# Block 2 of a two-block transformer kernel: scores of split q and k taken earlier, av projected last, two evictions moved to ScalarE

## The chip, the cores and the metric

One core of one Trainium2 chip runs the whole program. The metric is the time of one execution on the device, in microseconds. PE is TensorE, DVE VectorE, ACT ScalarE, POOL GpSimd and SP the engine whose queue issues the weight loads.

## The reference

Two blocks of two layers each work on x (512 tokens, 1024 features), in float32. The first block is not touched by the change. A layer of the second block is, cut to what matters:

```python
def hybrid_layer(x, mem, norm_g, w_in, w_out, mem_norm_g, w_mem_kv, qk_g):
    h = rms_norm(x, norm_g)
    proj = jnp.einsum('btd,de->bte', h, w_in)
    a_q, a_k, a_v, a_g, b_q, b_k, b_v, b_g, m_q, m_g = jnp.split(proj, cuts, axis=-1)
    qa = rope(rms_norm(to_heads(a_q, 6), qk_g[0])); ka = rope(rms_norm(to_heads(a_k, 6), qk_g[1]))
    oa = from_heads(moba_attention(qa, ka, to_heads(a_v, 6)))      # causal at 512 tokens
    ...                                                            # b: dilated, 6 heads, the same
    m_k, m_v = jnp.split(rms_norm(mem, mem_norm_g) @ w_mem_kv, 2, axis=-1)
    om = from_heads(memory_attention(qm, km, to_heads(m_v, 4)))    # 256 memory rows, 4 heads
    y = jnp.concatenate([oa * silu(a_g), ob * silu(b_g), om * silu(m_g)], axis=-1)
    return x + jnp.einsum('bte,ed->btd', y, w_out)
```

A head has 64 features. Scores are q k^T / 8 with a mask, then softmax, then times v.

## The kernel before

Every engine has its program written out by hand, and semaphores join them. There is no scheduler: what an engine does next is the next line of its own loop.

**Projections.** Each weight group (aq, ak, av, bq, bk, bv, mq, ag, bg, mg, and the two halves of out) has 8 steps of 128 input features. A step takes one slot of a ring of 4 (`RING`): SP loads the raw weights, ACT rounds them to w_hi (`round_weights`, L1021), DVE subtracts to w_lo (`residue`, L1343), and PE does three float32r passes (hi by hi, hi by lo, lo by hi) for each of the 2 to 4 banks of the group (`step`, L695). ACT and DVE run up to 3 steps ahead (`AHEAD`) and then wait for PE to free a slot. A group's banks have to be read (evicted) before the next group starts in them.

**Order of the projections in block 2.** `block_2` of PE projects aq, ak, av, bq, and then bk with `gemm_led`, which puts the first events of the attention (`a.lead`) between its steps. DVE works on the heads of aq and ak (norm, rotation: `head_norm`, `rotate`, L1442) beside av and bq, evicts ak and bq, and, within the attention, bv and mq (L1383). ACT evicts aq, av, bk (L1059) and the gates ag, bg, mg.

**Attention of block 2.** `Stream` holds its order. There are 8 pairs of heads: 3 of moba (a), 3 of dilated (b), 2 of memory. A pair has 4 units, one for each 128 queries: unit i of a causal pair has i + 1 blocks of 128 keys, one of memory always has 2. A unit takes 1 or 2 steps of two key blocks, so a causal pair has 6 steps, a memory pair 4, and the whole 44. In a step PE does the events of `begin`, then its share of the projections still to do (bv, mq, ag, bg, mg, 5 steps of out: `side`), then, at a pair's first step, the product with v of the pair before (`values`, L791), then the transposes of the step's probabilities (`turn_probs`, L779), for which there is one PSUM bank (T_BANK).

The events are: `turn`, where PE transposes q and k of a pair into banks 0 and 1 (L750) and DVE copies them out (L1478, L1482); `scores`, where PE multiplies them into the same two banks, one a head (L762), DVE masks and takes the maximum (L1498), and ACT takes the exponential (L1068); and `scale`, where DVE multiplies by the inverse sum (L1510). Scores of a unit come two steps ahead of its first step, and there are 3 buffers of probabilities.

The scores are plain float32 matmuls over all 128 rows: `kT_2` holds each head's k in its own 64 rows, with zeros (written once by POOL) in the other 64, and q of both heads stands in qT. A float32 matmul stands in the trace as two records.

## Time and profile before

| what | us |
|---|---|
| three runs | 1687.91, 1688.66, 1690.15 |
| median | 1688.66 |
| the profiled execution | 1690.31 |
| its span in the trace | 1688.5 |
| its mean granted clock | 0.993 of full speed |

The profile is of one execution. Its page gives the busy time of the engines and the costliest groups of instructions. Other views give the same for a stretch of time, list who waited for whom, or show the instructions in order of time. A busy time counts overlapping matmuls once in a stretch but each in full in a group, since the end of a matmul is modelled; what a matmul takes of PE's time is read from one start to the next. Block 2 runs from about 1070 us to the end, its first layer up to about 1385 us.

### The profile page before, as it was taken

Reading aid. Unit: us, or ns where it says so; the run is one execution under the profiler, and the core shown is the slowest. Engines: PE = TensorE matmul, PEld = TensorE weight load, DVE = VectorE, ACT = ScalarE, POOL = GpSimd, SP = SyncE. Lnnn points to the kernel's source line nnn. Section 1 sums busy time; section 2 is a strip of 40 time slices with the busy share of each in tenths; the row PEclk is TensorE's granted clock in tenths of the full one; section 3 lists DMA queues with packets and bytes.
Section 4 is the critical chain, followed back from the end, with each engine's and each line's share of the span. In section 5 each row is a group of like instructions: output and inputs, shape, how many; then the busy total and the mean of one; then the engine's idle time right before and its main releaser. Section 6 shows DMA issues by size and latency. Waiting matters only on the chain.

```text
span 1688.5 us, 21496 instructions
## 1 busy us (share of the span) xinstructions
PE 1618.3 (96%) x8009; PEld 1326.6 (79%) x8009; DVE 1005.9 (60%) x2246; ACT 729.7 (43%) x1503; POOL 57.8 (3%) x80
## 2 busy tenths in 40 slices
PE   6999999999999999999999999999989999998999
PEld 6878777788887878777788887999767789985667
DVE  4597656444444397757443344486876554788663
ACT  4444443333234443543332434434456553354662
POOL 0000002000001000002000001000000010000000
PEclk9999999999999999999999999999999999999999
DMA  6332121323323223112233323332112233211121
GB/s 219 93 92 71 42 63 51 100 88 100 100 94 96 85 87 88 51 50 63 76 96 92 99 90 110 104 88 60 57 38 69 76 95 92 83 56 38 38 76 62
DMA packets 80883, 136.23 MB, mean 81 GB/s; under 512 B 8190, under 2 KB 33420, under 8 KB 80780
## 3 DMA queue, kind: packets, MB, share of 16 engines
q1 hardware_dynamic: 77264, 129.48, 25.7%
q10 hardware_dynamic: 3516, 5.37, 1.0%
q8 instruction: 64, 1.05, 0.3%
q14 instruction: 39, 0.32, 0.1%
HBM read 132.74 MB, written 2.10 MB: 80 GB/s over the span
## 4 chain that ended last, share of the span: by engine, by line
PE 46%; DVE 13%; ACT 4%; issue 2%; POOL 0%; ACTq 0%; DVEq 0%
PE gemm_bank L695 35%; PE aux_bank L762 3%; PE aux_bank L791 3%; DVE w_lo L1343 2%; PE aux_bank L779 2%; DVE rope L1442 1%; DVE head_sums L1395 1%; ACT w_hi L1021 1%; DVE probs L1498 1%; ACT probs L1068 1%; DVE kT L1482 1%; PE aux_bank L750 1%; DVE probs L1510 1%; ACT L1296 0%; PE aux_bank L939 0%
## 5 line engine op out<-in xcount | busy, mean ns | idle before, releaser
L1021 ACT ACTIVATE w_hi<-raw 128x512 fp32r<-128x512 f32 (+3 forms) x524 | 305.5, 587 | 673.3 <-PE gemm_bank L695 671.9
L1343 DVE TENSOR_TENSOR w_lo<-raw,w_hi 128x512 fp32r<-128x512 f32 (+3 forms) x524 | 329.9, 636 | 441.9 <-ACT w_hi L1021 440.2
L695 PE MATMUL gemm_bank<-act_hi,w_hi 128*128 128x512 f32 x768 | 316.7, 412 | 10.9 <-DVE mq_flat L1383 3.7
L695 PE MATMUL gemm_bank<-act_hi,w_lo 128*128 128x512 f32 x768 | 300.2, 391 | 0.0
L695 PE MATMUL gemm_bank<-act_lo,w_hi 128*128 128x512 f32 x768 | 299.9, 391 | 0.0
L695 PE MATMUL gemm_bank<-w_hi,act_hi 128*128 128x384 f32 (+3 forms) x736 | 269.3, 366 | 6.4 <-DVE bq L1383 2.9
L695 PE MATMUL gemm_bank<-w_lo,act_hi 128*128 128x384 f32 (+3 forms) x736 | 257.2, 349 | 0.0
L695 PE MATMUL gemm_bank<-w_hi,act_lo 128*128 128x384 f32 (+3 forms) x736 | 257.2, 349 | 0.0
L695 PEld LDWEIGHTS gemm_bank<-act_hi,w_hi 128*128 128x128 f32 x768 | 144.6, 188 | 47.9 <-issue 12.7
L695 PEld LDWEIGHTS gemm_bank<-act_lo,w_hi 128*128 128x128 f32 x768 | 144.8, 189 | 31.9 <-issue 2.9
L695 PEld LDWEIGHTS gemm_bank<-act_hi,w_lo 128*128 128x128 f32 x768 | 144.5, 188 | 31.0
L695 PEld LDWEIGHTS gemm_bank<-w_hi,act_hi 128*128 128x128 f32 x736 | 139.2, 189 | 24.2 <-issue 10.0
L695 PEld LDWEIGHTS gemm_bank<-w_lo,act_hi 128*128 128x128 f32 x736 | 139.2, 189 | 11.3 <-issue 1.9
L695 PEld LDWEIGHTS gemm_bank<-w_hi,act_lo 128*128 128x128 f32 x736 | 138.8, 189 | 9.7
L762 PE MATMUL aux_bank<-kT,qT 128*128 128x256 f32 (+7 forms) x384 | 121.4, 435 | 5.8 <-DVE kT L1482 4.8
L1082 ACT ACTIVATE probsT<-aux_bank 128x256 f32<-128x256 f32 (+1 forms) x136 | 71.9, 529 | 114.7 <-PE aux_bank L779 113.9
L1068 ACT ACTIVATE probs<-probs,neg_max 128x128 f32<-128x128 f32 (+2 forms) x192 | 104.2, 544 | 35.6 <-DVE neg_max L1498 35.2
L779 PE MATMUL aux_bank<-ident,probs 128*128 128x128 f32 x464 | 76.1, 280 | 14.3 <-DVE probs L1510 14.2
L762 PEld LDWEIGHTS aux_bank<-kT,qT 128*128 128x128 f32 (+1 forms) x384 | 64.3, 194 | 27.3 <-DVE kT L1482 9.2
L779 PEld LDWEIGHTS aux_bank<-ident,probs 128*128 128x128 f32 x464 | 56.5, 142 | 36.9 <-DVE probs L1510 21.0
L695 PE MATMUL gemm_bank<-y_hi,w_hi 128*128 128x512 f32 x192 | 74.8, 390 | 0.3 <-ACT gate L1201 0.3
L695 PE MATMUL gemm_bank<-y_hi,w_lo 128*128 128x512 f32 x192 | 74.7, 389 | 0.0
(289 smaller groups left out, 2132.7 us busy)
## 6 DMA issues: line engine op xcount, KB each, us to landing
raw<-in_w_in SPq DMA_DIRECT2D x104, 512.0 KB, 3.5
raw<-in_w_in SPq DMA_DIRECT2D x64, 384.0 KB, 3.3
raw<-in_w_out SPq DMA_DIRECT2D x32, 512.0 KB, 3.7
raw<-in_w_branch SPq DMA_DIRECT2D x24, 512.0 KB, 3.7
raw<-in_w_mem_kv SPq DMA_DIRECT2D x8, 512.0 KB, 3.8
raw<-in_w_in SPq DMA_DIRECT2D x16, 256.0 KB, 2.8
raw<-in_w_in SPq DMA_DIRECT2D x8, 416.0 KB, 4.8
x<-in_x SPq DMA_DIRECT2D x4, 512.0 KB, 5.2
```

The costliest lines, as they stand in the source:

```text
L695: last = pe.matmul(o, a, c, start=begin and n == 0, stop=end and n == 2)
L750: last = pe.transpose(bank[0:kind.rows, t * P:(t + 1) * P], of(h, t), ident[:, :])
L762: pe.matmul(bank[:, 0:n_keys * P], a.qT_of(g, x)[:, i * P:(i + 1) * P], a.kT_of(g, x)[:, 0:n_keys * P], start=True, stop=True).then_inc(fu ...
L779: last = pe.transpose(bank[:, c:c + P], probs[a.where][m % 3][:, x, j * P:(j + 1) * P], ident[:, :])
L791: last = pe.matmul(bank[x * HD:(x + 1) * HD, kind.first_i(j) * P:T], kind.v_of(a.head(g, x), j), a.probsT_of(g, x, j), start=(j == 0), sto ...
L1021: act.activation(w_hi[:, s % RING, 0:n], raw[:, p % RAW, kk % PIECE, 0:n], ACT.Copy)\
L1068: act.activation(rows, rows, ACT.Exp, bias=neg_max[:, c:c + 1], scale=-1.0, accum_out=row_sum[:, c:c + 1]).then_inc(probs_ready, 1)
L1082: act.activation(a.turned_to(m, j0, j1), bank[:, 0:2 * (j1 - j0) * P].rearrange("p (x j s) -> p x j s", x=2, s=P), ACT.Copy)\
L1343: dve.tensor_tensor(w_lo[:, s % RING, 0:n], raw[:, p % RAW, kk % PIECE, 0:n], w_hi[:, s % RING, 0:n].bitcast(F32), ALU.subtract).then_inc( ...
L1395: dve.tensor_reduce(head_sums[:, c:c + heads], sq[:, n % 2, 0:heads, 0:d], AX_X, ALU.add)\
L1442: mark(dve.tensor_tensor(tmp[i][:, :, :, :], xx, t4, ALU.mult))
L1482: ins = dve.tensor_copy(a.kT_of(g, x + hh)[r, 0:kind.k_tiles * P], bank[r, 0:kind.k_tiles * P])
```

## The change

1. **Scores.** ACT rounds the transposed q and k of a pair from PSUM into `q_hi` and `k_hi` (`turned_hi`), DVE subtracts to `q_lo` and `k_lo` (event `low`, one step after `turn`), both float32r. PE does three float32r passes for each head, each over the head's own 64 rows (`scores_2`), the two heads taking turns. `kT_2`, its zeros and the semaphore `keys_zeroed` go.
2. **Two units at once.** Units 0 and 1 of a causal pair, and each two units of a memory pair, put their scores side by side in one bank (`together`).
3. **When.** Scores of block 2 come 4 steps ahead (`SCORES_LEAD`), or as soon as their buffer of probabilities is free; there are 4 buffers. `turn` moves to other steps.
4. **Projections.** The order is aq, ak, bq, bk, av; the lead events stand in av (turn in its step 3, scores in 5). DVE and ACT begin on the heads of b beside av.
5. **Evictions.** bq, bv and mq are evicted by ACT, not by DVE.

```diff
-        two("av", 2 * WA, WA)
         two("bq", 4 * WA, WB)
         two("bk", 4 * WA + WB, WB)
+        two("av", 2 * WA, WA)
...
             for m, mine in enumerate(self.steps_of):
                 self.begin[mine[0]].insert(0, ("scale", m))
-                if mine[0] >= 2:
-                    self.begin[mine[0] - 2].append(("scores", m))
+                if mine[0] >= 2 and self.together(m):
+                    last = max(self.together(m)) - self.buffers
+                    free = self.steps_of[last][-1] + 1 if last >= 0 else 0
+                    self.begin[max(mine[0] - SCORES_LEAD[block], free, 0)].append(("scores", m))
...
-        a.lead = {4: [("turn", 0, 0)], 5: [("scores", 0)], 6: [("scores", 1)]}
-        for g, (at_pair, step) in {1: (0, 1), 2: (0, 3), 3: (2, 1), 4: (2, 3), 5: (3, 3), 6: (4, 3), 7: (5, 3)}.items():
+        a.lead = {3: [("turn", 0, 0)], 4: [("low", 0, 0)], 5: [("scores", 0)]}
+        for g, (at_pair, step) in {1: (0, 0), 2: (0, 5), 3: (1, 5), 4: (2, 5), 5: (3, 5), 6: (4, 5), 7: (5, 4)}.items():
...
+        def scores_2(a, m):
+            g, kind = m // NT, a.kind(m)
+            if m % NT == 0:
+                aux_wait_read(pe, a.key("q", g, 0))
+                aux_wait_read(pe, a.key("k", g, 0))
+            banks = [aux_open(a.key("S", m, x), S_BANKS[x]) for x in range(2)]
+            for mm, c in a.together(m).items():
+                i, keys = mm % NT, kind.n_keys(mm % NT) * P
+                for n, (qq, kk) in enumerate(((q_hi, k_hi), (q_lo, k_hi), (q_hi, k_lo))):
+                    for x in range(2):
+                        r = slice(x * HD, (x + 1) * HD)
+                        last = pe.matmul(banks[x][:, c:c + keys], qq[r, g % 2, i * P:(i + 1) * P],
+                                         kk[r, g % 2, 0:keys], start=n == 0, stop=n == 2)
+                        if n == 2 and mm == max(a.together(m)):
+                            last.then_inc(full_of(a.key("S", m, x)), 1)
...
+        def turned_hi(a, g):
+            for what, hi in (("q", q_hi), ("k", k_hi)):
+                bank = aux_wait_full(act, a.key(what, g, 0))
+                n = T if what == "q" else a.pairs[g][0].k_tiles * P
+                act.activation(hi[:, g % 2, 0:n], bank[:, 0:n], ACT.Copy).then_inc(turned_hi_ready, 1)
...
+            for n, (what, hi, lo) in enumerate((("q", q_hi, q_lo), ("k", k_hi, k_lo))):
+                key = a.key(what, g, 0)
+                columns = T if what == "q" else a.pairs[g][0].k_tiles * P
+                dve.wait_ge(turned_hi_ready, 2 * a.turn_count(g) - 1 + n)
+                dve.tensor_tensor(lo[:, g % 2, 0:columns], aux_bank[aux_place[key][0]][:, 0:columns],
+                                  hi[:, g % 2, 0:columns].bitcast(F32), ALU.subtract).then_inc(read_of(key), 1)
...
+                elif name in ("bv", "mq"):
+                    evict_now(gi, ACT.Copy, lambda b: flat_2(name)[:, b, :])
```

**PE where the attention starts** (first layer: last matmuls of the led projection, then step 0). `aq` and `ak` are the operands of the second pair's turn. Before:

```order
L695 MATMUL gemm_bank<-w_lo,act_hi 128x384
L695 MATMUL gemm_bank<-w_hi,act_lo 128x384
L762 MATMUL aux_bank<-kT_177,qT_175 128x384 x2
L695 MATMUL gemm_bank<-w_hi,act_hi 128x384
L695 MATMUL gemm_bank<-w_lo,act_hi 128x384
L695 MATMUL gemm_bank<-w_hi,act_lo 128x384
L695 MATMUL gemm_bank<-w_hi,act_hi 128x384
```

and the turn of the second pair, a step later, behind the first transposes of probabilities:

```order
L695 MATMUL gemm_bank<-w_lo,act_hi 128x384
L695 MATMUL gemm_bank<-w_hi,act_lo 128x384
L779 MATMUL aux_bank<-ident,probs_181 128x128 x2
L750 MATMUL aux_bank<-ident,aq 128x128 x4
L750 MATMUL aux_bank<-ident,ak 128x128 x4
L695 MATMUL gemm_bank<-w_hi,act_hi 128x384
```

Now:

```order
L717 MATMUL gemm_bank<-w_lo,act_hi 128x384
L717 MATMUL gemm_bank<-w_hi,act_lo 128x384
L803 MATMUL aux_bank<-k_hi,q_hi 128x384 x2
L803 MATMUL aux_bank<-k_hi,q_lo 128x384 x2
L803 MATMUL aux_bank<-k_lo,q_hi 128x384 x2
L803 MATMUL aux_bank<-k_hi,q_hi 128x512 x2
L803 MATMUL aux_bank<-k_hi,q_lo 128x512 x2
L803 MATMUL aux_bank<-k_lo,q_hi 128x512 x2
L772 MATMUL aux_bank<-ident,aq 128x128 x4
L772 MATMUL aux_bank<-ident,ak 128x128 x4
L717 MATMUL gemm_bank<-w_hi,act_hi 128x384
L717 MATMUL gemm_bank<-w_lo,act_hi 128x384
```

The scores of unit 2 (384 keys), those of unit 3 (512 keys) and the second pair's turn now stand behind each other with nothing between; all three use banks 0 and 1.

**DVE at the end of the heads of a** (first layer; `ISA` of L1452, now L1512, tells PE that the heads are ready; `sq` holds the squares of heads of b). Before:

```order
L1447 TENSOR_TENSOR ak<-rope_170,rope_171 128x24x32
L1452 ISA
L1343 TENSOR_TENSOR w_lo<-raw,w_hi 128x384 x3
L1383 COPY bq<-gemm_bank 128x384 x4
L1343 TENSOR_TENSOR w_lo<-raw,w_hi 128x384 x4
L1478 COPY qT_175<-aux_bank 128x512
L1482 COPY kT_177<-aux_bank 64x512 x2
L1343 TENSOR_TENSOR w_lo<-raw,w_hi 128x384
```

Now:

```order
L1507 TENSOR_TENSOR ak<-rope_170,rope_171 128x24x32
L1512 ISA
L1403 TENSOR_TENSOR w_lo<-raw,w_hi 128x384 x4
L1455 TENSOR_REDUCE head_sums<-sq_172 128x6
L1403 TENSOR_TENSOR w_lo<-raw,w_hi 128x384
L1455 TENSOR_REDUCE head_sums<-sq_172 128x6
L1403 TENSOR_TENSOR w_lo<-raw,w_hi 128x384
L1455 TENSOR_REDUCE head_sums<-sq_172 128x6
L1403 TENSOR_TENSOR w_lo<-raw,w_hi 128x384
L1455 TENSOR_REDUCE head_sums<-sq_172 128x6
L1546 TENSOR_TENSOR q_lo<-aux_bank,q_hi 128x512
L1546 TENSOR_TENSOR k_lo<-aux_bank,k_hi 128x512
```

The eviction of bq and the three copies of q and k are gone, the sums of the heads of b have come in between, and two subtractions stand where the copies were.

**ACT within the attention** (first layer, around the end of the projection mq). Now:

```order
L1064 ACTIVATE w_hi<-raw 128x384 x2
L1120 ACTIVATE probs_185,row_sum<-probs_185,neg_max 128x384 x2
L1137 ACTIVATE probsT_188<-aux_bank 128x2x2x128
L1102 ACTIVATE mq_flat<-gemm_bank 128x256 x4
L1064 ACTIVATE w_hi<-raw 128x384
L1108 ACTIVATE q_hi<-aux_bank 128x512
L1108 ACTIVATE k_hi<-aux_bank 128x512
L1137 ACTIVATE probsT_188<-aux_bank 128x2x256
```

Before, `mq_flat` was DVE's to write, and ACT had neither `q_hi` nor `k_hi`: its rows at the next gate, for comparison, were

```order
L1082 ACTIVATE probsT_185<-aux_bank 128x2x256
L1021 ACTIVATE w_hi<-raw 128x384
L1068 ACTIVATE probs_183,row_sum<-probs_183,neg_max 128x384 x2
L1082 ACTIVATE probsT_185<-aux_bank 128x2x128
L1296 ACT_TABLE_LOAD
L1296 ACTIVATE agT<-gemm_bank 128x512 x3
L1021 ACTIVATE w_hi<-raw 128x384
L1082 ACTIVATE probsT_185<-aux_bank 128x2x2x128
```

The eviction of mq and the rounding of the next pair's q and k now stand ahead of the copy of the step's transposed probabilities.

## Rows read from the trace of the kernel before

**Rows 1.** the page: its span, and the busy time of each engine (us, share, instructions)
```profile
span 1688.5 us, 21496 instructions
PE 1618.3 (96%) x8009; PEld 1326.6 (79%) x8009; DVE 1005.9 (60%) x2246; ACT 729.7 (43%) x1503; POOL 57.8 (3%) x80
```

**Rows 2.** sums by stretch: PE, weight load, DVE, ACT, POOL busy (x count), granted clock
```profile
1180.00:1240.00 60.00, 52.39 (x301) 41.06 (x301) 53.06 (x154) 25.47 (x71) 0.00 (x0) 0.97 0.17 53
1240.00:1300.00 60.00, 57.31 (x290) 40.58 (x288) 39.84 (x117) 37.94 (x88) 0.00 (x0) 1.00 0.16 45
...
1070.00:1688.50 618.50, 582.77 (x3114) 484.91 (x3112) 405.35 (x1059) 294.36 (x694) 5.58 (x14) 0.99 0.23 68
```

**Rows 3.** waits of PE from 1070 us to the end: total us, times, longest
```profile
PE aux_bank L779 <- DVE probs L1510: 12.2, 10, 2.0
PE aux_bank L762 <- DVE kT L1482: 4.8, 10, 0.8
PE gemm_bank L695 <- DVE mq_flat L1383: 3.7, 2, 2.7
...
PE gemm_bank L695 <- DVE bq L1383: 2.9, 2, 1.5
...
PE gemm_bank L695 <- DVE bv L1383: 1.6, 2, 0.8
PE aux_bank L762 <- DVE qT L1478: 1.0, 2, 0.5
```

**Rows 4.** timeline of PE: start, us, line, operation, count; f32 scores, then projection matmuls
```profile
1179.40 1.03 PE L762 MATMUL aux_bank<-kT,qT 128*128 128x256 f32 x4
...
1180.44 0.34 PE L695 MATMUL gemm_bank<-w_lo,act_hi 128*128 128x384 f32 x1
1180.61 0.34 PE L695 MATMUL gemm_bank<-w_hi,act_lo 128*128 128x384 f32 x1
...
1190.86 0.28 PE L695 MATMUL gemm_bank<-w_hi,act_lo 128*128 128x256 f32 x1
...
1191.21 0.28 PE L695 MATMUL gemm_bank<-w_hi,act_lo 128*128 128x256 f32 x1
...
1241.49 0.40 PE L695 MATMUL gemm_bank<-act_lo,w_hi 128*128 128x512 f32 x1
...
1241.95 0.39 PE L695 MATMUL gemm_bank<-act_hi,w_hi 128*128 128x512 f32 x1
```

**Rows 5.** timeline of PE: matmuls with 64-row operands in two halves of the array
```profile
269.29 2.88 PE L929 MATMUL aux_bank<-vc,ks_tok 64*128 64x256 f32 x16 [0.52 <-DVE att L1866]
```

**Rows 6.** timeline of PE: into and out of matmuls with a 16-row operand
```profile
237.31 0.60 PE L779 MATMUL aux_bank<-ident,probs 128*128 128x128 f32 x4
237.84 1.98 PE L857 MATMUL aux_bank<-g_T,w_gu 16*128 16x512 f32 x4
239.74 0.50 PE L695 MATMUL gemm_bank<-w_hi,act_hi 128*128 128x512 f32 x1
240.08 0.40 PE L695 MATMUL gemm_bank<-w_lo,act_hi 128*128 128x512 f32 x1
```

**Rows 7.** groups of DVE, 1070 to 1380 us: count, busy us, mean ns, idle before
```profile
L1482 DVE COPY kT<-aux_bank 64x512 f32<-64x512 f32 x12 | 8.2, 684 | 0.2
L1478 DVE COPY qT<-aux_bank 128x512 f32<-128x512 f32 x8 | 5.5, 686 | 2.6 <-PE aux_bank L750 2.6
L1536 DVE TENSOR_TENSOR x<-gemm_bank,x 128x512 f32<-128x512 f32 x8 | 5.2, 687 | 5.2 <-PE gemm_bank L695 5.2
L1442 DVE TENSOR_TENSOR rope<-bq,table 128x768 f32<-128x768 f32 x4 | 3.6, 951 | 0.0
...
L1383 DVE COPY bq<-gemm_bank 128x384 f32<-128x384 f32 x4 | 1.9, 548 | 0.0
```

**Rows 8.** groups of ACT in the same stretch
```profile
L1082 ACT ACTIVATE probsT<-aux_bank 128x512 f32<-128x512 f32 x32 | 18.8, 589 | 16.8 <-PE aux_bank L779 16.5
...
L1059 ACT ACTIVATE av<-gemm_bank 128x384 f32<-128x384 f32 x4 | 2.0, 492 | 0.1
```

161 lines of the change are left out of this document (89 added, 72 removed).

## The prediction

> **What bounds the kernel now.** I read the page first: PE is busy 1618 of 1688.5 us [rows 1], so a change pays where it takes work off PE or ends a wait of PE. Only block 2 changes, so next comes its stretch, from 1070 us to the end: PE is busy 583 of 618.5 us, and DVE 405 and ACT 294 have room on average [rows 2]. Not everywhere: from 1180 to 1240 us, where DVE rotates the heads of b beside the attention, DVE is busy 53 of 60 us and PE only 52, while in the 60 us after that DVE has 40 and PE 57 [rows 2]. The list of PE's waits names what is late: probabilities that DVE has yet to scale (12.2 us), copies of turned q and k (4.8 + 1.0), evictions by DVE of mq (3.7), bq (2.9) and bv (1.6) [rows 3]. These are 26 us of the 36 in which PE is idle. So there are two places to gain, PE's work and some 26 us of waits, and both go straight to the end, since PE is the chain.
>
> **The scores, before.** Four float32 records of 256 columns (one unit, two heads) and one projection matmul of 384 columns start within 1180.44 - 1179.40 = 1.04 us, and such a projection matmul takes 0.17, so the unit takes 0.87 us, 0.217 a record [rows 4]. It scales with columns. Six causal pairs have 1280 key columns each (128 + 256 + 384 + 512), two memory pairs 1024: 9728 a layer, 38 times 256. Two layers: 76 x 0.87 = 66 us.
>
> **The scores, after.** Float32r matmuls of projections start 0.117 us apart at 256 columns (three in 0.35 us), 0.173 at 384 and 0.23 at 512; transposes with 128 columns and a weight load each, 0.11 [rows 4, 6]. If the two heads, in different halves of the array's rows, run at the same time, three pairs of matmuls take: units 0 and 1 together 3 x 0.11 + 3 x 0.117 = 0.68 us, unit 2 0.52, unit 3 0.69, two memory units 0.70. A layer: 6 x 1.89 + 4 x 0.70 = 14.1; both 28 us.
>
> Do they run together? The trace has one case: 16 float32 records of 256 columns over 64 rows, four in one half, four in the other, and so on, take 2.88 us to the modelled end [rows 5]. One after another they would take 16 x 0.217 plus some 0.16 of tail, 3.6. The 0.75 saved is a whole record at each of the three changes of half, all that this order allows. In the new order the half changes with every matmul, so I take full overlap as likeliest.
>
> **Going in and out of half-array matmuls** has a price. Four transposes of 0.11 us, then four records over 16 rows of 2 x 0.213 us, then one projection matmul of 0.23, would take 0.44 + 1.71 + 0.23 = 2.38 us; from 237.31 to 240.08 they take 2.77 [rows 6]. So 0.4 us a visit. The change makes 3 visits for a causal pair and 2 for a memory pair, 22 a layer, 44 x 0.4 = 17.6 us. The bound below is 0 (all of it hidden by a wait that was there anyway). The Trainium skill's page "TensorEngine Tiling (Array Packing)", Key Properties, says that changing the tiling mode drains TensorE. By that rule, which speaks against this change, each visit costs, and the 0.4 us of the trace agrees with it.
>
> Sum for the scores: 66 - 28 - 17.6 = 20 us gained.
>
> **Waits that go.** (a) bq: after the change ACT evicts it, with nothing in front, where DVE had three w_lo of the next group first; 2.9 us go. (b) The copies of q and k: the turn now stands a step or more ahead of its scores, so rounding (ACT, 2 x 0.59 us [rows 8]) and subtraction (DVE, 2 x 0.69, as for other reads of PSUM with a second operand [rows 7]) have a step of about 4.7 us; 5.8 go. (c) bv and mq, 5.3: ACT evicts them where it now evicts gates. It reads bank 0 while PE fills the others, but exponentials may be in front of it; I leave 1.0, so 4.3 go. (d) Scaled probabilities, 12.2: the longer lead doesn't help where DVE is behind with everything, and the rotation (eight products of 0.95 us a layer [rows 7], and as much again in sums) still lies in 4 steps of the attention, now steps 4 to 8 instead of 9 to 12. DVE has there about 3.8 us of rotation, 1.8 of scores and scaling and 1.2 of w_lo in a step for which PE takes 5. Over a layer DVE gets 10 us lighter: 15.4 of copies (12 x 0.684, 8 x 0.686 and four short ones [rows 7]) and 5.2 of evictions go, 10.5 of subtractions come. I take a quarter, 3.2 us, and leave 9.
>
> **A wait that comes.** At step 0 PE now does the scores of unit 2, of unit 3, and the second pair's turn back to back, all in banks 0 and 1. Behind unit 2's scores PE waits for DVE to read both banks, 2 x 0.6 us plus 0.2 to get there; behind unit 3's for 0.7 + 0.2 until bank 0 is read, and 0.3 more for bank 1 behind the q transposes. With the ends of the matmuls some 2.9 us a layer, 5.8 in all; everything behind it on PE waits too, the fill first, and nothing covers it. Later pairs have two steps between any two users of these banks.
>
> **What costs nothing.** ACT gets 14.4 us a layer (roundings 14 x 0.59 + 2 x 0.38, evictions 8 x 0.49 + 4 x 0.38 [rows 8]). Its fullest stretch has 38 of 60 us [rows 2] and would have 42 of 60: the cover is ACT's slack. POOL's zeros were not waited for. The weight loads of SP keep their sizes and only swap places. Without that cover see rival 3.
>
> **Sum.** -20.2 (scores) - 2.9 - 5.8 - 4.3 - 3.2 + 5.8 = -30.6 us. Against the profiled execution's own 1690.3 us this is 1659.7; it stood 1.6 above the median of the three runs, so **1658 us**, 1.8% faster.
>
> **The rivals.**
>
> 1. *The two heads don't overlap in the array* (float32r over 64 rows could behave otherwise than the float32 of [rows 5]). Then a layer's scores take 6 x 3.78 + 4 x 1.40 = 28.3 us, 57 in two, and with the visits 74 where 66 were: 8 lost instead of 20 gained, 1686 us. For it: no row shows alternation. Against: three changes of half, each with full overlap. 8%.
>
> 2. *Weight loads of the two heads follow each other.* Every matmul has its own load, and no row shows load and matmul of 128 columns below 0.11 us [rows 6]. If two heads' loads can't overlap, a pair of matmuls takes at least 0.22: units 0 and 1 1.32 us, unit 2 0.66, unit 3 0.69, two of memory 1.32, 42.6 us in two layers. The scores then gain 6 instead of 20: 1672 us. For it: one bus could feed both. Against: in [rows 5] the overlap included the loads. 15%. The Trainium skill's page "TensorE: Matmul & The Clock Gate", LDWEIGHTS (loading the stationary operand), lets a load's time go by its columns whatever its rows, at 128 columns 107 ns; a load of 64 rows would be no cheaper, which is what this rival needs, while the trace's 0.11 agrees with the price.
>
> 3. *ACT becomes late, and the kernel slower.* There is one bank for transposed probabilities, so PE's transposes of each step wait for ACT's copy of the step before. Ahead of that copy ACT now has, in some steps, four exponentials at once, two roundings or an eviction. If ACT falls behind by more than a step, PE waits in most of 88 steps; from 0.35 us a step (30.6 / 88) the change loses. At 0.4 us a step it is 35 us: 1693. Against: ACT has 18 of 60 us free even where it is fullest. 7%.
>
> 4. *DVE sets the pace for the first ten steps.* Whatever PE saves there (about a quarter of the scores' gain and of the waits, 7 us a layer) turns into longer waits for scaled probabilities or for w_lo: 1672 us. For it: 53 of 60 us [rows 2], and the rotation in one piece. Against: DVE is 10 us lighter. 14%.
>
> 5. *All goes well*: the 9 us left for probabilities vanish and half the visits are hidden: 1640 us. 6%.
>
> **How the numbers follow.** The forecast has 50%. Its own range is 1648 (visits half free) to 1666 (the start's wait and those for probabilities both 4 us worse). Range: rivals 2 and 4 are taken in, with some room above for both of them at once; 1 and 3, 15%, stay out above, and the far part of 5 below: 1644 to 1681. What this kernel's measurement can tell from no change is about 0.2%, 3.4 us. Faster than 1685.3: forecast, rivals 2, 4 and 5, and a part of 1: 0.88. Within 0.2%: most of 1, 0.05. Slower: 3, and 1 with some of 3, 0.07.
>
> **What the profile after would show.** Right: records of the new score line in pairs that start within some 0.01 us, pairs 0.11 to 0.23 us apart; from the last matmul before such a group to the first after it 0.4 us more than the columns need; no waits of PE for evictions by DVE or for turned q and k; two waits of about 1.4 and 1.1 us at step 0 of each layer; DVE's busy time 20 us lower, ACT's 29 higher; the granted clock no lower than 0.99. Wrong: pairs spread by 0.11 (rival 2) or by their columns (rival 1), PE's transposes waiting for ACT's copy of probsT (rival 3), or more than 12 us of waits for scaled probabilities (rival 4).

## The result, and the profile after

The changed kernel is slower. Its median is **1700.3 us** (1699.0 to 1702.1, four runs) against 1688.7 for the kernel before on the same chip: ratio 1.0068, 95% interval 1.0051 to 1.0086. The forecast was 1658, its range ended at 1681, and 0.07 was left for slower. The profiled execution has 1701.4 us and a span of 1699.6.

The page of the changed kernel, its first lines:

```profile
span 1699.6 us, 21791 instructions
...
PE 1603.0 (94%) x8137; PEld 1315.9 (77%) x8137; DVE 983.7 (58%) x2206; ACT 750.9 (44%) x1559; POOL 55.5 (3%) x79
```

Beside [rows 1] PE has 15 us less work, DVE 22 less, ACT 21 more (20 less and 29 more were forecast for the last two). The work of PE and DVE went about as forecast, ACT's by less, and the span the other way, so the time is in waits. The waits of PE from 1070 us to the end (total us, times, longest), to be laid beside [rows 3]:

```profile
PE aux_bank L803 <- DVE k_lo L1546: 26.5, 12, 5.4
PE aux_bank L822 <- DVE probs L1576: 20.0, 14, 2.1
PE aux_bank L803 <- DVE neg_max L1559: 3.8, 2, 2.5
PE aux_bank L822 <- ACT probsT L1137: 3.3, 6, 0.8
PE gemm_bank L717 <- ACT bgT L1355: 2.1, 2, 1.1
...
PE aux_bank L772 <- DVE neg_max L1559: 1.5, 2, 0.8
```

The evictions of bq, bv and mq are gone from the list. The wait for turned q and k has grown from 5.8 to 26.5 us, that for scaled probabilities from 12.2 to 20.0. The sums by stretch (columns as in [rows 2]) show that no engine is short of time there:

```profile
1180.00:1240.00 60.00, 49.36 (x325) 40.29 (x325) 39.48 (x107) 28.80 (x79) 0.00 (x0) 0.94 0.16 51
1240.00:1300.00 60.00, 48.36 (x273) 34.32 (x270) 37.76 (x122) 33.91 (x82) 0.00 (x0) 0.98 0.14 42
...
1070.00:1688.50 618.50, 559.23 (x3208) 467.47 (x3207) 380.52 (x1016) 315.17 (x750) 5.56 (x14) 0.97 0.22 66
```

DVE has 39 of 60 us where it had 53, and still PE waits for it more. The stretches don't hold quite the same work, since the rotation now begins earlier, but in 20 us pieces too DVE's fullest piece of the attention (1200 to 1220 us) has 16.6 us of work. Now the longest of the twelve waits for k_lo in order of time (start, us, engine, line, idle time before and its releaser; PE's projection matmuls left out):

```profile
1185.47 0.60 PE L772 MATMUL aux_bank<-ident,aq 128*128 128x128 f32 x4
...
1185.90 0.60 PE L772 MATMUL aux_bank<-ident,ak 128*128 128x128 f32 x4
...
1188.95 0.60 PE L822 MATMUL aux_bank<-ident,probs 128*128 128x128 f32 x4
1189.01 0.58 ACT L1108 ACTIVATE q_hi<-aux_bank 128x512 fp32r<-128x512 f32 x1
1189.14 0.42 DVE L1403 TENSOR_TENSOR w_lo<-raw,w_hi 128x256 fp32r<-128x256 f32 x1 [2.04 <-ACT w_hi L1064]
1189.48 3.56 DVE L1502 TENSOR_TENSOR rope<-bq,table 128x768 f32<-128x768 f32 x4
...
1193.54 0.68 DVE L1546 TENSOR_TENSOR q_lo<-aux_bank,q_hi 128x512 fp32r<-128x512 f32 x1
1194.14 0.68 DVE L1546 TENSOR_TENSOR k_lo<-aux_bank,k_hi 128x512 fp32r<-128x512 f32 x1
...
1194.97 0.80 PE L803 MATMUL aux_bank<-k_hi,q_hi 64*128 64x512 f32 x2 [5.42 <-DVE k_lo L1546]
```

The turn ends at 1186.5. ACT rounds q 2.5 us later, since the weights of the step come first and wait for a free slot of the ring. DVE stands idle 2.04 us for the same weights, then does w_lo and 3.56 us of rotation, and only then, at the start of its next step, the subtraction. PE has ended its step at 1189.55; its next begins with the scores of the last unit, which go into the banks that the turn has filled. It stands there 5.42 us, to 1194.97.

### The profile page after: what moved, and what is told of

Same layout as the page of the kernel before. It is cut to its first block, busy times and chain, and to the rows that moved or that the text cites. A ratio compares the mean times of both kernels' runs of the same rounds, so it can differ in the third digit from the quotient of the medians.

```text
span 1699.6 us, 21791 instructions
## 1 busy us (share of the span) xinstructions
PE 1603.0 (94%) x8137; PEld 1315.9 (77%) x8137; DVE 983.7 (58%) x2206; ACT 750.9 (44%) x1559; POOL 55.5 (3%) x79
## 4 chain that ended last, share of the span: by engine, by line
PE 46%; DVE 12%; ACT 4%; issue 2%; POOL 0%; ACTq 0%; DVEq 0%
PE gemm_bank L717 36%; PE aux_bank L834 3%; DVE w_lo L1403 2%; PE aux_bank L822 2%; PE aux_bank L803 2%; DVE rope L1502 2%; ACT w_hi L1064 1%; ACT probs L1120 1%; PE aux_bank L787 1%; PE aux_bank L772 1%; DVE probs L1576 1%; DVE probs L1559 1%; DVE head_sums L1455 1%; DVE q_lo L1546 0%; ACT probsT L1137 0%
## 5 line engine op out<-in xcount | busy, mean ns | idle before, releaser
L717 PE MATMUL gemm_bank<-act_hi,w_hi 128*128 128x512 f32 x768 | 312.3, 407 | 8.5 <-ACT u L1102 3.5
L717 PE MATMUL gemm_bank<-y_lo,w_hi 128*128 128x512 f32 x192 | 74.7, 389 | 0.0
L1576 DVE TENSOR_SCALAR probs<-probs,row_inv 128x128 f32<-128x128 f32 (+2 forms) x192 | 64.5, 379 | 3.4
```

Source lines behind the costliest of these rows:

```text
L717: last = pe.matmul(o, a, c, start=begin and n == 0, stop=end and n == 2)
L1576: ins = dve.tensor_scalar(rows, rows, row_inv[:, c + x:c + x + 1], None, ALU.mult)
```

## The experiments

All ran with the kernel before on the same chip; its medians were 1688.4 to 1689.8. "Waits" are PE's from 1070 us to the end, in one profiled execution each, in us. "Half" is how long the trace's clock records grant half of full speed (1.2 of 2.4 GHz) after 1070 us. It is that of the profiled execution; executions of one kernel differ in it (mean granted clock 0.986 to 0.991 in the four of e2), so a few us of it between two kernels say little. Intervals of kernels less than about 4 us apart overlap (e11 and e9, e15 and e6). The diff of an experiment that is built on another shows only what it adds.

| kernel | median | ratio, interval | q, k | probs | probsT | masks | ACT's evictions | half |
|---|---|---|---|---|---|---|---|---|
| before | 1688.7 | | 5.8 | 12.2 | 3.1 | 0 | 0.9 (DVE's 8.2) | 10 |
| changed | 1700.3 | 1.0051-1.0086 | 26.5 | 20.0 | 3.3 | 5.3 | 2.1 | 34 |
| e1 low in the step of turn | 1677.7 | 0.992-0.995 | 1.9 | 22.0 | 3.3 | 5.3 | 5.6 | 21 |
| e2 last unit a step later | 1678.3 | 0.9923-0.9956 | 12.2 | 13.9 | 7.1 | 5.2 | 2.1 | 18 |
| e3 head by head | 1700.7 | 1.0052-1.0082 | 26.4 | 19.4 | 2.5 | 5.2 | 2.1 | 38 |
| e4 before, ACT evicts bv, mq | 1680.4 | 0.9933-0.9962 | 5.9 | 11.0 | 3.0 | 0 | 0.9 (DVE's 2.9) | 3 |
| e5 e1 + start spread | 1671.1 | 0.988-0.9909 | 2.4 | 19.6 | 3.0 | 0.8 | 5.5 | 18 |
| e6 e1 + scale a step earlier | 1665.7 | 0.9845-0.9878 | 2.7 | 0 | 8.2 | 11.6 | 4.9 | 24 |
| e7 low behind the weights | 1688.4 | 0.9989-1.0008 | 12.3 | 23.2 | 1.7 | 5.3 | 2.1 | 31 |
| e8 e1 + memory heads later | 1674.8 | 0.9903-0.9932 | 6.4 | 15.3 | 1.7 | 5.3 | 5.5 | 27 |
| e9 e5 + e6 + e8 | 1659.1 | 0.9807-0.9843 | 10.6 | 0 | 6.3 | 2.1 | 5.5 | 14 |
| e10 e9, copy first | 1666.1 | 0.9848-0.988 | 10.8 | 0 | 2.0 | 5.9 | 8.4 | 21 |
| e11 e9, roots in pieces | 1656.4 | 0.979-0.9821 | 3.3 | 0 | 3.5 | 2.1 | 3.6 | 17 |
| e12 before, scale earlier | 1686.4 | 0.9973-0.9992 | 11.6 | 0 | 2.8 | 2.8 | 0.9 (DVE's 10.8) | 7 |
| e13 e11, memory heads only | **1652.5** | 0.9764-0.9796 | 7.3 | 0 | 6.3 | 2.1 | 5.5 | 7 |
| e14 e1 with two steps of lead | 1668.8 | 0.9859-0.9888 | 7.2 | 12.3 | 4.9 | 0 | 8.9 | 7 |
| e15 e14 + scale earlier | 1662.7 | 0.9829-0.9858 | 13.3 | 0 | 6.8 | 0.4 | 8.9 | 10 |

### e1: q and k read in the step of their turn

```diff
-                at = [event[0] for event in self.begin[step + 1]].index("scores") \
-                    if "scores" in [event[0] for event in self.begin[step + 1]] else len(self.begin[step + 1])
-                self.begin[step + 1].insert(at, ("low", g, x))
+                self.begin[step].append(("low", g, x))
...
         def attention(a, evict_beside, extra):
             for n, (m, j0, j1) in enumerate(a.steps):
-                split_beside(split, a, n, evict_beside)
                 for event in a.begin[n] if a.block == 2 else ():
                     if event[0] == "turn":
                         turned_hi(a, event[1])
+                split_beside(split, a, n, evict_beside)
```

> The changed kernel with one thing else: q and k of a pair are read out of banks 0 and 1 in the very step in which PE turns them. ACT rounds them ahead of its weights of that step, and DVE's two subtractions stand ahead of its w_lo and its rotation of that step, not at the start of the next step. Theory: in the changed kernel PE's 26.5 us of waits for k_lo come from the place of the subtraction; turn and the next user of the banks (scores of the last unit) are only one step of about 4 us apart, and that step's w_lo, rotation and rounding stand in front. Then the waits for k_lo fall from 26.5 to under 5 us, those for scaled probabilities stay at about 20, and the time falls from 1700.3 to 1672 - 1679. Rival: DVE has too much to do in these steps whatever the order; then the 26 us come back as waits for scaled probabilities or w_lo (together above 40 us), and the time stays at 1693 - 1700.

1677.7 us, 22.6 less than the changed kernel, by moving two small groups of instructions. PE's longest waits, e1:

```profile
PE aux_bank L820 <- DVE probs L1574: 22.0, 16, 2.1
...
PE aux_bank L801 <- DVE k_lo L1544: 1.9, 3, 0.8
```

The 26.5 us are 1.9. Of the 24.6 that went, 5.5 came back elsewhere: 3.5 at ACT's evictions of mq and bg, whose programs now have the rounding in front, and 2.0 at scaled probabilities. The rival wanted all of them back, so the change's loss is the place of rounding and subtraction, not DVE's load; which of the two places counts for what, e7 asks. With e1 the change is faster than the kernel before, by 11 us.

### e2: the scores of the last unit one step later

```diff
-                    self.begin[max(mine[0] - SCORES_LEAD[block], free, 0)].append(("scores", m))
+                    late = block == 2 and m % NT == 3 and self.kind(m).name != "memory"
+                    self.begin[max(mine[0] - SCORES_LEAD[block], free, 0) + late].append(("scores", m))
```

> The changed kernel, but the scores of the last unit of each causal pair come one step later (three steps ahead of their use, not four). No instruction is added or dropped. Turn and these scores are then two steps apart, and DVE's subtraction stays where it is, at the start of the step between. Theory (one step is too short for the place where the subtraction stands): waits for k_lo fall from 26.5 to under 8 us, the two waits at step 0 go as well since the second pair's turn no longer stands behind these scores (3 us), time 1673 - 1681. Rival (DVE has too much to do): 1693 - 1700, the waits turning up at scaled probabilities.

1678.3 us, in the theory's band, but not all by its way: it wanted under 8 us of waits for k_lo and none for masks, and 12.2 and 5.2 are left, while those for probabilities fell by 6.1, which it had not named. Here the subtraction keeps its place and the next user of the banks moves away. Of the 12.2 us that stay, 11.7 are two waits of 5.85 us at the first pair of each layer, where I had moved those scores to step 1, one step behind the second pair's turn at step 0. Where turn and scores are two steps apart the wait is gone, and where they are one step apart it is there. e1 and e2 give the same answer from the two sides.

### e3: head by head

```diff
-                for n, (qq, kk) in enumerate(((q_hi, k_hi), (q_lo, k_hi), (q_hi, k_lo))):
-                    for x in range(2):
+                for x in range(2):
+                    for n, (qq, kk) in enumerate(((q_hi, k_hi), (q_lo, k_hi), (q_hi, k_lo))):
```

> The changed kernel with the three passes of one head behind each other and then the three of the other, in place of heads taking turns. Same matmuls, same columns. Theory (the two heads run at the same time in the changed kernel, which is where its 20 us came from): now only one of six matmuls can run beside another, so the scores take about 5/3 of 28 us: +19 us of PE work. Part of it lies where PE waits anyway behind the scores, so 1710 - 1721, and starts of matmuls in a unit stand 0.11 to 0.23 us apart instead of in pairs. Rival (the heads did not overlap, or the order makes no difference to the array): 1698 - 1703.

1700.7 us: no difference from the changed kernel, where the theory wanted 10 to 20 more. PE's timeline for a unit with 384 keys, the changed kernel:

```profile
1213.49 0.41 PE L822 MATMUL aux_bank<-ident,probs 128*128 128x128 f32 x2 [0.39 <-ACT probsT L1137]
1213.83 0.44 PE L803 MATMUL aux_bank<-k_hi,q_hi 64*128 64x384 f32 x2
1214.11 0.34 PE L803 MATMUL aux_bank<-k_hi,q_lo 64*128 64x384 f32 x2
1214.28 0.34 PE L803 MATMUL aux_bank<-k_lo,q_hi 64*128 64x384 f32 x2
1214.55 0.39 PE L717 MATMUL gemm_bank<-w_hi,act_hi 128*128 128x256 f32 x1
1214.77 0.28 PE L717 MATMUL gemm_bank<-w_lo,act_hi 128*128 128x256 f32 x1
1214.89 0.29 PE L717 MATMUL gemm_bank<-w_hi,act_lo 128*128 128x256 f32 x1
```

and the same unit in e3, where the program has the three matmuls of one head first:

```profile
1212.80 0.45 PE L803 MATMUL aux_bank<-k_hi,q_hi 64*128 64x384 f32 x2
1213.08 0.34 PE L803 MATMUL aux_bank<-k_hi,q_lo 64*128 64x384 f32 x2
1213.25 0.34 PE L803 MATMUL aux_bank<-k_lo,q_hi 64*128 64x384 f32 x2
1213.53 0.38 PE L717 MATMUL gemm_bank<-w_hi,act_hi 128*128 128x256 f32 x1
```

Both heads run at the same time in both (six matmuls of 384 columns in 0.72 and 0.73 us; the two of a pair start 2 to 3 ns apart in the one, 9 to 10 in the other). So the experiment doesn't tell overlap from none by the time; the starts show the overlap directly. But the rival's "the order makes no difference to the array" was right, and my assumption about the order was wrong.

### e4: the kernel before, with ACT evicting bv and mq

```diff
+                elif group_key[gi][2] in ("bv", "mq"):
+                    evict_now(gi, ACT.Copy, lambda b: flat_2(group_key[gi][2])[:, b, :])
...
-            attention(a, out_2, evict_tokens, beside_steps, drain)
+            attention(a, out_2, None, beside_steps, drain)
```

> The kernel before with one part of the change: bv and mq are evicted by ACT within the attention, not by DVE. Theory (term (c) of the prediction): the waits for these evictions, 5.3 us, shrink to about 1, and with DVE 2.6 us a layer lighter the waits for scaled probabilities don't grow: 1688.7 becomes 1683 - 1685. Rival: on ACT they stand in front of exponentials, and PE waits for probabilities or for the copy of the transposed ones instead: 1687 - 1691.

1680.4 us, 8 less, more than the theory's 4 to 5. Both waits are gone and that for probabilities fell by 1.2, but 2.2 us of a new one came (the turn waiting for the heads of b): 4.3 less in the whole list (27.9 of 32.2 us), as the theory has it. Half-clock time fell from 10 to 3 us, worth up to 3.4, and that is where most of the rest of the 8 can come from; the mean granted clock was 0.994 to 0.996 in all four runs and 0.993 in the seven of the kernel before beside them.

### e5: the start spread out (on e1)

```diff
-                    self.begin[max(mine[0] - SCORES_LEAD[block], free, 0)].append(("scores", m))
+                    if block == 1 or m != 2:
+                        self.begin[max(mine[0] - SCORES_LEAD[block], free, 0)].append(("scores", m))
...
-        a.lead = {3: [("turn", 0, 0)], 4: [("low", 0, 0)], 5: [("scores", 0)]}
+        a.lead = {3: [("turn", 0, 0)], 4: [("low", 0, 0)], 5: [("scores", 0)], 7: [("scores", 2)]}
-        for g, (at_pair, step) in {1: (0, 0), 2: (0, 5),
+        for g, (at_pair, step) in {1: (0, 1), 2: (0, 5),
...
             evict(gi, ACT.Copy, lambda b: flat_2("av")[:, b, :])
+            exponentials(a, 2)
```

> The kernel with q and k read in the step of their turn (first experiment, 1677.7 us), and the start spread out: the scores of the third unit come in the last step of the led projection av, those of the last unit in step 0, the second pair's turn in step 1. No instruction is added. Theory: PE's 5.3 us of waits for neg_max (the two at step 0 of each layer) go, and with them the half-clock spells beside them at 1160 and 1470 us (3.4 us each, worth half of that): 1669 - 1673. Rival: ACT has then four exponentials in front of the evictions and weights of step 0, and DVE two masks more beside the led projection; PE's wait moves to w_lo or to the first probabilities: 1675 - 1680.

1671.1 us, 6.6 less, as the theory has it. The waits for masks at step 0 fall from 5.3 to 0.8, those for probabilities by 2.4, and the half-clock spell at 1160 us is gone; one at 1472 us stays.

### e6: the scaling one step earlier (on e1)

```diff
-                self.begin[mine[0]].insert(0, ("scale", m))
+                self.begin[mine[0] - 1 if block == 2 and m else mine[0]].append(("scale", m))
...
+            for events in self.begin:
+                events.sort(key=lambda event: event[0] != "scale")
```

> The first experiment's kernel (1677.7 us), and DVE scales the probabilities of a unit one step earlier, still in front of the masks of that step. Nothing else moves; the exponentials of every unit were done two to three steps earlier. Theory: the 22.0 us of waits for scaled probabilities are no lack of DVE time but its order: the scaling stands in the step that needs it, behind the small operations of the head norms, the gates and w_lo of the step before, some of which wait for ACT. Four steps of lead for the scores bring nothing while the scaling keeps its place. Then these waits fall from 22.0 to under 8 us and the time to 1660 - 1668. Rival: DVE is short of time there; the waits stay above 15 us and the time at 1673 - 1680.

1665.7 us, 12.0 less, within the theory's band. PE's waits, e6:

```profile
PE aux_bank L822 <- ACT probsT L1137: 8.2, 8, 2.3
PE aux_bank L772 <- DVE neg_max L1559: 6.5, 6, 2.0
PE aux_bank L803 <- DVE neg_max L1559: 5.1, 2, 3.3
```

No wait for scaled probabilities is left of 22.0 us. About half came back as waits for ACT's copy (+4.9) and for masks (+6.3), which now stand behind the scaling.

### e7: only in the right step, behind the weights (on the changed kernel)

```diff
-                at = [event[0] for event in self.begin[step + 1]].index("scores") \
-                    if "scores" in [event[0] for event in self.begin[step + 1]] else len(self.begin[step + 1])
-                self.begin[step + 1].insert(at, ("low", g, x))
+                self.begin[step].append(("low", g, x))
...
                 for event in a.begin[n] + a.middle.get(n, []):
...
-                    else:
+                    elif event[0] != "low":
                         begin(a, *event)
                 split_beside(split, a, n, evict_beside)
+                for event in a.begin[n]:
+                    if event[0] == "low":
+                        begin(a, *event)
```

> The changed kernel (1700.3 us) with DVE's two subtractions in the step of the turn, but behind that step's w_lo, and with ACT's order left as it is in the changed kernel (weights first, then rounding of q and k). It tells whether one needs to be in front of the weights, or only in the right step. Theory: w_lo of a step waits for PE to free a slot of the ring, so the subtraction comes in the middle of PE's step; about 1.5 us of each of the ten waits stays: waits for k_lo 5 - 12 us, and the waits for evictions of mq and gates are those of the changed kernel (2.1, not 5.6): 1677 - 1686. Rival: what stands behind is the rotation and the heads' norms alone; then waits for k_lo under 3 us and 1673 - 1677, better than the first experiment.

1688.4 us, in ten runs. The wait for k_lo is 12.3 us, ten times up to 1.5, just past the theory's 5 to 12; the time is 2 us above its band, and the waits for probabilities grew by 3.2. The rival is refuted. So the rotation and the step's end made about half of the loss, the weights in front (on DVE and on ACT) the other half: with both out of the way it is 1677.7, with the first alone 1688.4, with neither 1700.3.

### e8: the memory heads' sums one step later (on e1)

```diff
-                for work in [b_heads] + [m_heads] * (n > n_m):
+                for work in [b_heads] + [m_heads] * (n > n_m + 1):
```

In e1, DVE's timeline shows why the probabilities are late there:

```profile
1222.57 0.75 DVE L1453 TENSOR_REDUCE head_sums<-sq 128x4 f32<-128x256 f32 x2 [4.27 <-ACT sq L1082]
...
1223.83 0.15 DVE L1570 RECIPROCAL row_inv<-row_sum 128x2 f32<-128x2 f32 x1
1224.02 0.62 DVE L1574 TENSOR_SCALAR probs<-probs,row_inv 128x256 f32<-128x256 f32 x2
...
1226.32 0.75 DVE L1453 TENSOR_REDUCE head_sums<-sq 128x4 f32<-128x256 f32 x2 [1.22 <-ACT sq L1082]
```

ACT makes the squares behind its copy of PE's transposes of the same step, so DVE's next scaling hangs on PE's present step.

> The first experiment's kernel (1677.7 us), and DVE begins with the sums of the memory heads one step later; ACT's squares stay where they are. In the first experiment DVE stands idle there (4.27 + 1.22 + 1.87 us from 1218 to 1232 us), waiting for squares that ACT makes only behind its copy of transposed probabilities, and PE then waits 1.48 and 0.81 us. Theory: these idle times go, and of PE's waits for probabilities 3 - 5 us in two layers: 1672 - 1675. Rival: the rest of the memory heads' work only moves to a step where it hurts as much: 1677 - 1680.

1674.8 us, 2.9 less, near the upper end of the theory's band; the intervals of e8 and e1 overlap a little, so the size is not sure. The waits for probabilities fall by 6.7, those for k_lo grow by 4.5.

### e9, e10, e11, e13: together, and two refinements

e9 has the edits of e1, e5, e6 and e8.

> The four moves that each paid off alone, together: q and k read in the step of their turn, the start spread out, the scaling one step earlier, the memory heads' sums one step later. Alone, over the first experiment's 1677.7 us, the last three gave 6.6, 12.0 and 2.9 us. Theory (they end different waits): 1656 - 1660. Rival (they free the same DVE time, and what one gives the other takes): 1662 - 1666.

1659.1 us, in the theory's band: the gains add up within 3 us (21.5 apart, 18.6 together).

e10 moves ACT's exponentials behind its copy:

```diff
-                for event in a.begin[n] + a.middle.get(n, []):
-                    if event[0] == "scores":
-                        exponentials(a, event[1])
+                def exps():
+                    for event in a.begin[n] + a.middle.get(n, []):
+                        if event[0] == "scores":
+                            exponentials(a, event[1])
+                if a.block == 1 or n == 0:
+                    exps()
                 bank = aux_wait_full(act, a.key("T", n))
...
                    .then_inc(read_of(a.key("T", n)), 1)
+                if a.block == 2 and n:
+                    exps()
                 extra(n)
```

> The combined kernel, and ACT makes the exponentials of a step behind its copy of the transposed probabilities, not ahead of it (step 0 apart). In the kernel with the earlier scaling PE waited 8.2 us for that copy, which stands behind up to four exponentials. Theory: the exponentials have two or three steps of room, the copy has none, so these waits fall to under 3 us: 4 - 6 us below the combined kernel. Rival: ACT then stands idle at the copy until PE's transposes, and the exponentials and squares come too late for DVE: the waits move to neg_max or probabilities, time as the combined kernel or up to 5 us above.

1666.1 us, 7 more than e9, where the rival had up to 5. The theory is refuted: the copy's wait fell from 6.3 to 2.0 as wanted, but the time did not; masks grew from 2.1 to 5.9 and ACT's own evictions from 5.5 to 8.4.

e11 cuts the inverse roots of the head norms into pieces, and e13 only those of the memory heads (`n == 24`):

```diff
             for _ in range(3):
+                if n in (24, 48):
+                    yield
                 settle()
                 mark(dve.tensor_tensor(z, y, y, ALU.mult))
```

> The combined kernel, and the chain of twelve small DVE operations for the inverse roots of the head norms (about 0.2 us each, 2.4 us in a piece) is cut into four pieces, two in each step. Theory: in the kernel with the earlier scaling PE waits 2.0 us a layer at the turn for masks that stand behind this chain, and some at step 2; 2 - 4 us below the combined kernel. Rival: later scaling of rows of the heads takes its place in the next steps: no change within 1.5 us.

> The combined kernel (1659.1 us) with the chain for the inverse roots cut into pieces for the memory heads alone; that of the heads of b stays in one piece. With both cut (1656.4 us) PE waited 3.96 us a layer at the turn of the first pair of b, for heads that were not ready. Theory: these 7.9 us go, and the other gains of cutting stay except at step 2: 1650 - 1654. Rival: what PE waited there would have been lost anyway, at k_lo or at the copy of transposed probabilities in the next steps: 1656 - 1659.

e11 took 1656.4 (2.7 less than e9) and e13 **1652.5 us**, the fastest here, 37 below the kernel before beside it (1689.8; ratio 0.978). A wait of e11 that e13 does not have:

```profile
PE aux_bank L773 <- DVEq L1516: 7.9, 2, 4.0
```

The heads of b were late for their first turn. In e13 these 7.9 us are gone, and 1.9 at w_lo, but 8.7 came back: at k_lo (3.3 to 7.3), at the copy (3.5 to 6.3) and at ACT's evictions (3.6 to 5.5). In waits the rival was right, PE's whole list is only 1.1 us shorter. The time fell by 3.9 us all the same, into the theory's band; half-clock time in the two traces went from 17 to 7 us, worth up to 5 (mean granted clock 0.989 to 0.991 in the four runs of e11, 0.992 to 0.994 in those of e13), and that can be where most of it comes from. So the theory's number came in by another way than its own.

### e12: the kernel before, with the scaling one step earlier

The edit is that of e6, in the kernel before.

> The kernel before, with one thing else: DVE scales the probabilities of block 2 one step earlier. Scores keep their lead of two steps. Theory (the waits for scaled probabilities come from the scaling's place, and needed no longer lead): the 12.2 us of waits fall to under 5, 1688.8 becomes 1679 - 1683. Rival: with two steps of lead the exponentials are only just done, DVE then waits for ACT and holds up masks and copies of q and k: 1686 - 1692. Then the longer lead is what makes the earlier scaling possible.

1686.4 us, only 2.4 less: the rival. The 12.2 us of waits for probabilities are gone, but the others grew by 11. DVE's waits (1150 to 1340 us) have one that the kernel before doesn't have:

```profile
DVE row_inv L1508 <- ACT probs L1070: 6.0, 9, 2.0
```

In this kernel, two steps ahead, the exponentials are only just done when DVE wants to scale, and w_lo, masks, copies and the eviction of mq (3.7 to 6.9 us of PE's waits) queue behind it.

### e14, e15: a lead of two steps in the new kernel

```diff
-    SCORES_LEAD = {1: 2, 2: 4}
+    SCORES_LEAD = {1: 2, 2: 2}
...
-        for g, (at_pair, step) in {1: (0, 0), 2: (0, 5), 3: (1, 5), 4: (2, 5), 5: (3, 5), 6: (4, 5), 7: (5, 4)}.items():
+        for g, (at_pair, step) in {1: (0, 1), 2: (0, 3), 3: (2, 1), 4: (2, 3), 5: (3, 3), 6: (4, 3), 7: (5, 3)}.items():
```

e14 has this on e1, e15 on e6.

> The first experiment's kernel (1677.7 us) with the scores two steps ahead and the turns in the steps where the kernel before has them; split scores, two units at once, the new order of projections and ACT's evictions stay. Theory: the longer lead by itself brings nothing, since the scaling keeps its place in the step that needs it; DVE's work is the same and its order little changed: 1674 - 1680, waits for probabilities about 20 us. Rival (the lead does give the scaling room): exponentials are only just done when DVE comes to scale, waits for probabilities 28 us or more: 1684 - 1692.

> The kernel of e14 with the scaling one step earlier; that is e6 (1665.7 us) with a lead of two steps in place of four. Theory (the kernel before with earlier scaling gained only 2.4 us because DVE then waited 6.0 us a layer for ACT's exponentials): the same here; DVE waits for exponentials and holds up masks, subtractions and w_lo, so only 2 - 4 us of the 12 that e6 gained are gained over e14: 1671 - 1677. Rival: with the lead of two it gains as much as with four: 1662 - 1668; then four steps are needed for nothing.

e14 took 1668.8 us, below both bands: with the scaling left in its place, the lead of four steps and the steps of the turns that belong to it cost 9 us together. The experiment moves both and doesn't part them. PE's waits, e14:

```profile
PE aux_bank L820 <- DVE probs L1574: 12.3, 14, 1.2
PE aux_bank L801 <- DVE k_lo L1544: 7.2, 8, 1.4
PE aux_bank L820 <- ACT probsT L1135: 4.9, 6, 1.1
PE gemm_bank L715 <- ACT bgT L1353: 4.6, 2, 2.3
```

The waits for masks at step 0 (5.3 us) don't arise, those for probabilities are 9.7 us less, others 10 more; in all 4.8 us less waiting, and 13 us less at half clock (up to 6.6). Much of the 9 us may stand at the start, where e5 won 6.6 with a lead of four.

e15 took 1662.7 us: the earlier scaling gives 6.1 us with a lead of two (theory 2 to 4, rival as much as with four) and 12.0 with four. The theory's reason is refuted too. DVE's waits in e15, 1150 to 1340 us:

```profile
DVE row_inv L1572 <- ACT probs L1120: 1.4, 4, 0.6
```

That is 1.4 us where e12 has 6.0: in the new kernel the exponentials are mostly done even with a lead of two. By the medians e15 is 3 us ahead of e6, but the two intervals overlap, so a lead of four is at best no better there. The kernels that are faster still (e9, e11, e13) have a lead of four, but also the start spread out and the memory heads later, and I did not try these with a lead of two. Whether the lead of four is worth anything is therefore not shown.

## Why the prediction was wrong

**The scores: right.** In sets that nothing disturbs, from the last transpose before them to the second projection matmul behind them, less what these two intervals take by themselves, units 0 and 1 take 1.09 us, unit 2 0.92, unit 3 1.09, two memory units 1.11. For unit 2 it can be read in the rows under e3: 0.72 us from 1213.83 to 1214.55, then 0.22 where the next projection matmul takes 0.12 (0.10 for coming out), and the two transposes before take 0.34 where they would take 0.22 (0.12; over all sets 0.09 for going in). Two layers: 46 us, against 28 + 17.6 forecast and 66 before. The 20 us were gained. Rivals 1 and 2 are refuted by the starts: the two matmuls of a pair start within 10 ns where nothing disturbs them, and units 0 and 1 take 0.89 us from the first start to the next projection matmul, where rival 2 has 1.32. One reason given for the overlap was wrong, though. The prediction took the 0.75 us saved in [rows 5] for all that the order of the program allows; e3 has an order of that kind and overlaps fully. So those rows showed a partial overlap, and that the new one is full was in part luck.

The starts of all matmuls after 1070 us, each interval put down to what begins and ends it, give the whole difference (us):

```
                                     before  changed     e1    e13
projection to projection              422.6    413.0  411.8  410.7
scores, to the next start              60.9     45.6   44.2   37.3
up to the first score                   9.6     36.2   11.2   18.0
up to and within probs' transposes     56.4     68.2   71.3   47.1
all else                               65.5     63.1   63.7   63.5
sum                                   615.0    626.1  602.2  576.6
```

(the first row has the evictions' waits and the exits from the scores in it; the second has the waits for masks between two units.)

**(a), bq: right**, the wait is gone. **(c), bv and mq: right**, and e4 shows it by itself: its list of waits is 4.3 us shorter, as forecast, and its time 8 us.

**(b), turned q and k: the step that failed.** It said that "the turn now stands a step or more ahead of its scores", so that rounding and subtraction "have a step of about 4.7 us", and, further down, "Later pairs have two steps between any two users of these banks." For the turns of the third to the seventh pair that is false: the next user of banks 0 and 1 is not the turned pair's own scores but the last unit's of the pair before, one step behind the turn. And the room is not a step: both readers stood behind weights that wait for PE to go on in that same step, and DVE's behind the rotation. Instead of 5.8 us gone, 20.7 came: 26.5 us of the 42 by which the forecast missed. e1, e2 and e7 show it. I had the order of DVE in hand, with the two subtractions at the start of the attention, where nothing stands between; I did not follow one of the later pairs.

**(d), scaled probabilities: wrong in sign.** 3.2 us were to go and 9 to stay; 7.8 came and 20.0 were measured, 11 us more than forecast. Of the reason, "the longer lead doesn't help where DVE is behind with everything", the first half was right, but DVE is not behind: it is idle (from 1130 to 1240 us 20.7 us for ACT's weights and 11.2 for ACT's squares), with the scaling in its queue behind them. e6 removes the waits by order alone, e8 a third of them. With lead and turns as in the kernel before they are 12.3 us against 22.0 (e14 and e1), so these two made them longer; by which of the two, and by which instructions, stays open.

**The wait that comes: right.** 5.8 us forecast, 5.3 measured (3.8 + 1.5), and e5 takes 4.5 of it away.

**ACT's cover held**: waits for its copy are 3.3 us, as before (3.1), and 2.1 for its evictions. Rival 3 is refuted as a cause. **Rival 4** named the right engine and the wrong reason: its sign, more than 12 us of waits for scaled probabilities, is there, but it gave them to DVE's load, and DVE had 21 of 60 us free where PE waited most.

**The clock** was forecast no lower than 0.99 over the run; it was 0.985 (0.993 before). Half-clock time after 1070 us went from 10 to 34 us, worth at most 12 us, less as far as PE stood still anyway. The falls stand at waits (see the last section), and the forecast had no term for them. In sum, against the 1659.7 us forecast for the profiled execution: 26.5 for (b), 11 for (d), and the 4 that are left of 42 are no more than the clock can explain. Sums of waits are not the same as time, as e1 and e13 show, so this account is good to a few us.

The Trainium skill's page "TensorEngine Tiling (Array Packing)", section Performance Considerations, warns that a faster TensorE leaves the reading of PSUM as it is, and that this may become the limit. I had taken from this page only the drain at a change of mode. What happened here is of that kind, though by order, not by load: ACT and DVE had room to read the banks, and read them too late.

## What to carry to other kernels

When a step is moved earlier, ask for each bank or buffer that it fills who uses it next, not who needs its result, and then what stands in the reader's queue between the two: above all instructions that themselves wait for the engine that is to be served. A longer lead is worth nothing by itself: here scores came four steps early and their scaling still stood in the step that needed it, and the kernel was 9 us slower than with a lead of two and its turns. Moving the scaling as well gained 12 us, but no run shows that the long lead was needed for the result. Before an engine is called full, look at its own waits: here 39 us of work in 60 and queue order were enough to make it late. And each move here brought some of its waits back at another place, so look at the whole list and not at the line that was to go.

## What the runs showed of the hardware that was not expected

- **The order of the two halves in the program did not matter.** In e3 the program has three matmuls of one half of the array and then three of the other, and they ran in pairs, about 10 ns apart, as if they took turns: the first of the second half started before the second of the first half (0.73 us for six of 384 columns, and 0.72 where the program alternates). The 16 float32 records in [rows 5] had overlapped much less; no run here shows why. The Trainium skill's page "TensorEngine Tiling (Array Packing)", Key Properties, says that different tiles can load weights and multiply in parallel, and the trace agrees.
- **Going into and out of half-array matmuls** cost 0.4 us a visit in all, as forecast from another kind of visit. In the rows under e3 the four parts can be read: the last transpose before takes longer to the next start (0.12 us there, 0.09 over all sets), the first pair by 0.11, the last pair 0.10 and the first projection matmul 0.10. Float32 matmuls have a tail too. In the kernel before, the first projection matmul behind a unit's scores takes 0.37 us to the next start, at 1180.44 [rows 4], where 0.17 is usual. Its row:

```profile
1180.07 0.52 PE L695 MATMUL gemm_bank<-w_hi,act_hi 128*128 128x384 f32 x1
```

  This tail grows with the columns: ahead of projections of 384 columns the interval is 0.26 us behind scores of 128 keys, 0.36 at 256, 0.47 at 384 and 0.58 at 512, so 0.09 to 0.41 more than 0.17. Scores and tail together take 0.45, 0.87, 1.30 and 1.73 us a unit, and so scale with the columns, as the prediction had it.
- **The granted clock falls at waits.** Every fall to half speed in block 2 of the changed kernel came within a wait of PE or less than 3 us behind one. By the clock records the first three begin at 1161.3, 1171.5 and 1192.0 us; waits of 2.53, 1.94 and 5.42 us ended at 1159.4, 1171.2 and 1195.0. Not every such wait has a fall. With the waits the falls mostly went: 34 us at half speed and 59 us of waits in the changed kernel, 21 and 40 in e1, 7 and 23 in e13. It is no fixed rate, since e14 has 7 us with 35 of waits. More than once the time fell by more than the waits did: e4 gained 8 us for 4.3 of waits. How much of that is the clock can't be told apart here.
